# Two trunk layers on one core: another DRAM layout for the S5 "inside" taps, and one table piece built four items later

## The reference, cut to what matters

```python
def s5_scan(u_g, h0, lam_re, lam_im, log_dt, b_re, b_im, c_re, c_im, reverse):
    ...
    bu = jnp.einsum("blgc,gpc->blgp", u_g.astype(jnp.complex64), b_bar)
    ...
    _, states = lax.associative_scan(ssm_combine, (a, bu), axis=1, reverse=reverse)
    y = jnp.real(jnp.einsum("gcp,blgp->blgc", c, states))
```

## Time and profile before

| | |
|---|---|
| median of 3 runs | 1577.14 us |
| the 3 runs | 1574.07, 1582.29, 1577.14 us |
| the profiled execution: its own time | 1574.07 us |
| its span (first to last instruction) | 1572.3 us |
| mean granted TensorE clock | 0.949 |
| TensorE busy | 1424.0 us (91%) |
| VectorE busy | 1042.4 us (66%) |
| 16 DMA engines, mean rate | 237 GB/s |

### The profile page before, as it was taken

One profiled execution on the slowest core, in us unless ns is written; L12 is line 12 of the kernel. 1 busy time (PEld: TensorE's weight loads), 2 busy tenths in 40 slices (PEclk: granted clock), 3 DMA queues, 4 the chain that ended last, 5 costly groups with the idle time before them and its releaser, 6 DMA issues. The chain is left out here.

```text
span 1572.3 us, 26708 instructions
## 1 busy us (share of the span) xinstructions
PE 1424.0 (91%) x10938; PEld 1299.6 (83%) x10938; DVE 1042.4 (66%) x1542; ACT 582.9 (37%) x680; POOL 35.2 (2%) x37
## 2 busy tenths in 40 slices
PE   5887699999999999999958477699999999999995
PEld 1865689889898988999958477699999999999995
DVE  7535477788877888887873744766565565565655
ACT  2434153333333333333331643533434334334342
POOL 2000100000000000000020000100000000000001
PEclk9979889999999999999978789899999999999998
DMA  9763478999999987877759665275565555555530
GB/s 363 273 223 105 160 249 300 333 335 334 325 322 330 350 292 277 290 274 276 246 161 298 263 196 188 90 260 195 198 213 186 209 204 189 214 194 198 213 135 27
DMA packets 149136, 372.96 MB, mean 237 GB/s; under 512 B 16792, under 2 KB 68280, under 8 KB 146624
## 3 DMA queue, kind: packets, MB, share of 16 engines
q1 hardware_dynamic: 149056, 371.87, 68.0%
HBM read 349.21 MB, written 21.50 MB: 236 GB/s over the span
## 5 line engine op out<-in xcount | busy, mean ns | idle before, releaser
L271 PE MATMUL PS<-moe_mod_HThl,moe_up_h 128*128 128x256 f32 x2080 | 591.8, 285 | 1.0 <-DVE moe_up_l L1614 1.0
L272 PE MATMUL PS<-moe_mod_HThl,moe_up_h 128*128 128x256 f32 x2080 | 588.6, 283 | 0.0
L273 PE MATMUL PS<-moe_mod_HThl,moe_up_l 128*128 128x256 f32 x2080 | 588.6, 283 | 0.0
L271 PEld LDWEIGHTS PS<-moe_mod_HThl,moe_up_h 128*128 128x128 f32 x2080 | 398.7, 192 | 14.9 <-issue 8.9
L272 PEld LDWEIGHTS PS<-moe_mod_HThl,moe_up_h 128*128 128x128 f32 x2080 | 398.8, 192 | 3.7
L273 PEld LDWEIGHTS PS<-moe_mod_HThl,moe_up_l 128*128 128x128 f32 x2080 | 398.9, 192 | 0.0
L1614 DVE TENSOR_TENSOR moe_up_l<-raw,moe_up_h 128x2048 fp32r<-128x2048 f32 x130 | 297.3, 2288 | 41.3 <-ACT moe_up_h L1603 41.2
L1619 DVE TENSOR_TENSOR moe_down_l<-raw,moe_down_h 128x1024 fp32r<-128x1024 f32 x130 | 159.2, 1225 | 173.2 <-ACT moe_down_h L1607 173.2
L1603 ACT ACTIVATE moe_up_h<-raw 128x2048 fp32r<-128x2048 f32 x130 | 246.9, 1901 | 11.0 <-DMA raw<-in_exp_w_down 11.0
L1607 ACT ACTIVATE moe_down_h<-raw 128x1024 fp32r<-128x1024 f32 x130 | 137.7, 1059 | 294.0 <-PE PS L273 294.0
L271 PE MATMUL PS<-moe_down_h,moe_hid_h 128*128 128x512 f32 x520 | 204.1, 392 | 0.0
(11 more groups left out here) (384 smaller groups left out, 1420.5 us busy)
## 6 DMA issues: line engine op xcount, KB each, us to landing
raw<-in_exp_w_gate SPq DMA_DIRECT2D x128, 512.0 KB, 3.8
raw<-in_exp_w_up SPq DMA_DIRECT2D x128, 512.0 KB, 5.2
raw<-in_exp_w_down SPq DMA_DIRECT2D x128, 512.0 KB, 6.3
side_slices<-in_ada_w SPq DMA_DIRECT2D x56, 512.0 KB, 8.5
moe_gate_b<-gate_rows SPq DMA_DIRECT2D x128, 128.0 KB, 3.3
part_slices<-in_ada_w SPq DMA_DIRECT2D x18, 512.0 KB, 6.4
raw<-in_ada_w SPq DMA_DIRECT2D x8, 1024.0 KB, 10.6
s_from_state<-G SPq DMA_DIRECT2D x16, 512.0 KB, 4.3
```

What stands on the lines that cost most here:

```text
L271: pe.matmul(out, ah, bh, start=start, stop=False, skip_group_check=True)
L272: pe.matmul(out, ah, bl, start=False, stop=False, skip_group_check=True)
L273: return pe.matmul(out, al, bh, start=False, stop=stop, skip_group_check=True)
```

## The change

Two things are changed. First, `kt_d` is laid out with the channel outermost, and the stores and the window loads follow it. In a store each partition's taps become one run of 8 KB (7 KB for the second half) in DRAM, where they were 8 (7) runs of 1 KB. In the window load each partition's eight taps become one run of 8 KB; the DRAM side's access pattern goes from [128 partitions, 8 taps, 256 numbers] to [8 taps, 16 channels, 2048 numbers]. The bytes moved and what lands where stay the same. Second, in `E_ITEMS` the fourth doubled item is 27 instead of 23.

```diff
-        kt_d = nc.dram_tensor("s5_inside_taps", [4, 15, C5, NAT * C5], F32, kind="Internal").ap()
+        kt_d = nc.dram_tensor("s5_inside_taps", [C5, 4, 15, NAT * C5], F32, kind="Internal").ap()
...
-            E_ITEMS = sorted(list(range(3, 31)) + [11, 15, 19, 23])
+            E_ITEMS = sorted(list(range(3, 31)) + [11, 15, 19, 27])
...
                 for q in range(4):
-                    kt = kt_d[q].rearrange("t c x -> c t x")
-                    sp.dma_start(kt[:, 0:CH, :], taps[32 * q:32 * q + C5, :, :]).then_inc(self.kt_stored, 16)
-                    sp.dma_start(kt[:, CH:2 * CH - 1, :], taps[32 * q + C5:32 * q + 2 * C5, 1:CH, :]).then_inc(self.kt_stored, 16)
+                    sp.dma_start(kt_d[:, q, 0:CH, :], taps[32 * q:32 * q + C5, :, :]).then_inc(self.kt_stored, 16)
+                    sp.dma_start(kt_d[:, q, CH:2 * CH - 1, :], taps[32 * q + C5:32 * q + 2 * C5, 1:CH, :]).then_inc(self.kt_stored, 16)
...
                             tap = NAT * C5
-                            windows = bass.AP(kt_d.tensor, q * 15 * C5 * tap, [[tap, P], [C5 * tap, CH], [1, tap]])
-                            sp.dma_start(home.rearrange("p (s x) -> p s x", s=CH), windows).then_inc(m_landed[q // 3], 16)
+                            windows = bass.AP(kt_d.tensor, q * 15 * tap, [[tap, CH], [4 * 15 * tap, C5], [1, CH * tap]])
+                            sp.dma_start(home, windows).then_inc(m_landed[q // 3], 16)
```

## The result

| | before | after |
|---|---|---|
| median, runs of one chip | 1578.89 us (4 runs, 1574.07 to 1582.29) | 1597.14 us (4 runs, 1596.32 to 1599.94) |
| profiled execution: own time, span | 1574.07, 1572.3 us | 1592.51, 1590.7 us |
| mean granted clock of TensorE | 0.949 | 0.941 |

The ratio is 1.0121, with a 95% interval of 1.009 to 1.0152: 1.2% slower. The forecast was 1580.5 us and "no change"; its range ended at 1587. The place and the order in which things came late were the ones forecast. The size was not: some 18 us where 3.4 were forecast. Of these 14.2 lie ahead of z, and that part has the size of rival B (+14.3).

What follows compares the result with a forecast made beforehand. TensorE was taken to bound the kernel, so only its waits count, decisively in layer 1's mixer. +3.9 for late z and -0.5 for the moved piece gave +3.4 on the median 1577.14: 1580.5 us, range 1573 to 1587.

Steps and rivals of the forecast that it cites:

- rival B: Window loads in layer 1's mixer on half the engines at a worse rate, 7.9 us each: +14.3 us, 1591; chance 0.05.
- What bounds the kernel: TensorE's waits for `rows(2)` (1.22 us) and `rows(3)` (0.36) behind the windows in layer 1's mixer; a microsecond lost there is the program's.
- The clock: TensorE's granted clock around z after the longer gap: taken as 0, bounds about +2.6 and -1.4 us.
- The stores of the taps: Eight DMAs with longer runs, covered by 3.9 us of VectorE's norm: cost nothing, at most 2.2 us to gain uncovered.
- inside(0..2): Three window loads in layer 1's mixer: on 8 engines at 210 GB/s, 5.0 us each instead of 3.0; bounds 2.5 and 7.9.
- What is late next: Queue behind the windows: `into(3)` 2.5 us behind them, then `rows(2)`, `rows(3)`; `chunks(2)` starts at 867.2, z +3.9 us.
- rival D: Engines are halved but `rows` overtakes the windows in the queue: 0, 1576.6 us; chance 0.05.
- inside(3): Fourth window load takes some 2 us longer, from-state loads behind it slip 2 us, covered by chunk steps: cost nothing.
- The moved piece: Doubled item 27 instead of 23 in the expert stage lightens the queue for weights: -0.5 us, range -0.5 to +2.7.
- rival C: Pieces stall VectorE behind item 27, and TensorE through the weights: +2.2 on +3.9, 1583.2, with clock 1586; chance 0.10.
- Rival A: Longer runs win on all 16 engines in the windows' queue; `rows(3)` keeps its floor: 1575.2 to 1576.6 us; chance 0.15.

Runs made afterwards that it cites:

- w1: Changed kernel, each window loaded as 128 plain 8 KB rows of the into-state table in one DMA on 16 engines; 1573.85 us beside 1579.03.
- y1: Changed kernel, each window as four DMAs of 32 partitions on 8 engines, from into-state table rows 64 KB apart; 200 GB/s, z 56.9 us from the mixer's start.
- x4: Changed kernel, windows read non-overlapping into-state table rows 64 KB apart, one DMA with 8 outermost as in the change; 1596.76 us in one run.
- v1: Changed kernel with its own window split (one DMA, 8 engines), but into-state table rows 960 KB apart; 144 GB/s, z 64.1 us from the mixer's start.
- w2: Changed kernel, each window as two DMAs of 64 partitions on 8 engines, into-state table rows 64 KB apart; 115 GB/s, z 66.7 us from the mixer's start.
- x2: Kernel before with only the new `E_ITEMS` list (fourth doubled item 27); 1577.23 us beside 1579.06, ratio 0.9998.
- x3: Changed kernel, each window as eight DMAs of 16 partitions, one per tap, on 16 engines, from the new layout; 1585.37 us beside 1581.02, ratio 1.0034.
- w3: Changed kernel, each window as eight DMAs of 16 partitions on 16 engines, into-state table rows 64 KB apart; 226 GB/s, z 52.6 us from the mixer's start.
- v3: Changed kernel, each window as eight DMAs of 16 partitions on 16 engines, into-state table rows 512 KB apart; 218 GB/s, z 52.6 us from the mixer's start.
- x6: Changed kernel with `into(3)`, `rows(2)` and `rows(3)` issued ahead of the windows `inside(0..2)`; 1598.7 us beside 1579.03, ratio 1.0103.
- u2b: Changed kernel, each window one DMA with 16 outermost, eight partitions per engine, into-state table rows 448 KB apart; 228 GB/s, z 52.6 us from the mixer's start.
- v2: Changed kernel, each window one DMA with 16 outermost, eight partitions per engine, into-state table rows 64 KB apart; 228 GB/s, z 53.6 us from the mixer's start.
- y3: Changed kernel, each window one DMA of the new layout's overlapping rows, 16 channels outermost, taps second; 1587.22 us beside 1579.06, ratio 1.0059.
- x5: Kernel before, old tap layout and 1 KB runs, window access pattern rewritten with 8 taps outermost; 1576.32 us in one run beside 1581.02.
- x8: Kernel before, layer 1 mixer's issues reordered: gate rows, scan tables and table tail later, windows behind `rows(3)`; 1577.7 us beside 1579.06, ratio 0.9981.

## Why the prediction was wrong

**What bounds the kernel**: right. The place where the time was lost is the wait for `rows(2)` behind the windows, and it went through to the end of the program in full.

**The clock** at nothing: right. After the wait of 18.05 us z's first products take 0.66 to 0.68 us, and they get to 0.41 at 887.55, 3.25 us behind z's start; before it was at 871.75, 3.29 behind it.

**The stores of the taps** at nothing: nothing in the trace speaks against it, and no run isolates them. w1, which has the new stores and the new list, speaks against a cost of theirs: 1573.85 us beside 1579.03, z 48.8 from start; but it is one run, and the four runs of before differ by 8 us.

**inside(0..2), 5.0 us each**: this is the step that failed, by its size. That the loads run on 8 engines was right (share 0.53). The size was not: the forecast took half of the 419 GB/s of a stretch with other transfers, 210, over the 133 GB/s of the one row with the same access pattern, and explained that row away as a tail in which some engines are through. It was no tail effect: the change's windows flow at 134 GB/s over 13 us on end, 7.8 us each. Two things were priced as one. Fewer engines cost a factor of 2; that is what y1 measures alone, and with z 56.9 from start even this is +7.7, not +3.9. So a second term was too small: under "What is late next" `into(3)` costs nothing but its own 2.5 us behind the windows, but while the two flow together all 16 engines are busy and slow, as in this stretch of y1:

```profile
854.00:857.00 3.00, 3.00 (x27) 2.87 (x25) 0.42 (x1) 0.00 (x0) 0.00 (x0) 1.00 1.05 221
```

The partitions that the engines write cost the rest: x4 has y1's engines and rows and the change's partitions, and loses 13.3 us in place of 7.7.

**What is late next**: the order was right in each step, windows, `into(3)`, `rows(2)`, `chunks(2)`, and rival D (`rows` overtakes) was not seen. In the time of before (less 1.64), `into(3)` landed at 877.2 and `chunks(2)` started at 878.1; rival B had 876.7 for the one and 879.6 for `chunks(3)`, and +14.3 where +14.2 came. Its chance was put at 0.05 with one reason against it, the runs of 8 KB; v1, w2 and x4 have runs of 8 KB and are about as slow (144, 115 and 163 GB/s). The reason was an argument, the 133 GB/s a measurement.

**inside(3)** at nothing, +2 us under cover: the transfer took 15.3 us from issue to use, 9.4 more than before, and TensorE's wait for it, 10.13 us, was still covered, for L2044 started 40.7 us after z in both. But the step named only the from-state loads as next in the queue. Those were in time; the weights of the output projection behind them were not, and cost 2.1 of the 2.6 us behind z, as far as these are more than scatter. What the other 0.5 is stays open.

**The moved piece** at -0.5: not measurable (ratio 0.9998 in x2, whose interval goes from -2.5 to +1.9 us and holds -0.5 as well as 0). VectorE's wait for its inputs (both tiles) grew from 3.9 us to 7.5, as step and rival C had it (6.4 in x2). The sign of rival C, TensorE waiting near 480 us, came in small: 1.86 us at 470. In x2 such waits are 1.5 us in all, and it is no slower.

**Rival A**: its bound was right. Full speed windows (w1) put z 0.5 us earlier than before, for `rows(3)` has its floor: even a layout that made the windows perfect had nothing to win here.

**Open**: why x3, w3 and v3 are no slower than two to a port, why the change's own overlapping rows are at 134 GB/s and x4's at 163, and why the engines that have no window to load slow down too (157 GB/s at 1.02 in x6). A window whose engines write 16 different ports, from the new table, was not tried: its rows can't be put as one plain pitch.

## What to carry to other kernels

Price a new transfer by the row whose access pattern has the same shape, even if it is short and mixed, before any row whose run length is the same; if you want to discard it, say what would have to be true and look for that. A DMA whose outermost dimension isn't the 128 partitions can lose twice: in the number of engines, and in which partitions they write at the same time; so read share and GB/s together, since a share of 1.02 with 228 GB/s is hardly faster than 0.5 with 200. And before changing how a load is laid out, ask what a perfect one would give: here a floor right behind it made that 0.5 us.

## What the runs showed of the hardware

- The same 16 engines, all busy, moved 8 KB pieces at 415 GB/s with 128 plain rows (w1) and at 228 with an outermost dimension of 16 over the same buffers (u2b, v2, y3).
- Eight engines moved them at 200 GB/s, 315 ns a piece, with four partitions to each (y1), and at 115 with eight (w2), though the bytes and the rows were the same.
- An access pattern that only reads as if it had 8 outermost (x5) ran like the 128 rows of before: 366 GB/s at 1.09.
- Issuing the three windows got cheaper by 8.62 - 1.96 = 6.7 us, with eight times fewer pieces; nothing waited for SyncE there, and it was worth nothing. The pieces are not all of it: in x8 the three windows of the old layout were issued in 3.34 us.
